# RWKV-7 chunk recurrence: the identity products of the state are taken out of TensorE, and VectorE adds a decayed copy of the state instead

## What is computed

```python
def step(s, inp):
    w_t, k_t, v_t, kk_t, a_t = inp[:5]
    sa = jnp.einsum('bhvk,bhk->bhv', s, kk_t)
    s = (s * w_t[:, :, None, :]
         - sa[..., None] * (kk_t * a_t)[:, :, None, :]
         + v_t[..., None] * k_t[:, :, None, :])
    y = jnp.einsum('bhvk,bhk->bhv', s, inp[5]) if len(inp) > 5 else None
    return s, y
```

## Time and profile before

| | us |
|---|---|
| median of three runs | 5098.99 (5093.28 to 5112.98) |
| profiled execution, its own time | 5105.09 |
| its span, first to last instruction | 5103.3 |
| around the span | 1.8 |
| granted TensorE clock, mean | 0.970 |
| TensorE busy (MATMUL) / weight loads | 4705.9 (92%) / 2817.4 (55%) |
| VectorE / ScalarE / GpSimd busy | 2535.0 (50%) / 1836.3 (36%) / 1383.1 (27%) |
| rwkv, 3107 to 4823 us: TensorE / VectorE busy | 1569.6 / 927.4 of 1716 |

### The profile page before, as it was taken

How to read it: one execution, slowest core, us unless ns; L and a number is a source line. 1 busy time by engine, 2 the same in 40 slices (tenths; PEclk the granted TensorE clock), 3 DMA queues, 4 the chain that set the end, 5 groups by cost and what they waited for, 6 DMA issues and landing times. The chain is left out here.

```text
span 5103.3 us, 123816 instructions
## 1 busy us (share of the span) xinstructions
PE 4705.9 (92%) x50814; PEld 2817.4 (55%) x50814; DVE 2535.0 (50%) x4204; ACT 1836.3 (36%) x4413; POOL 1383.1 (27%) x2884
## 2 busy tenths in 40 slices
PE   6999997999999998999999969899999989989699
PEld 3666663333333334454444437777787777778544
DVE  2444444665666661232343355555555555555376
ACT  1212111444444431132222225455555555555332
POOL 1111111333332320000000005444454444445343
PEclk8999997999999998999999989999999999999899
DMA  5222223000000005432322246666666666666575
GB/s 210 95 83 93 85 75 120 5 23 24 24 24 24 23 6 220 146 135 63 124 74 69 66 129 172 166 169 173 171 183 171 158 178 171 181 165 167 154 229 174
DMA packets 958460, 602.74 MB, mean 118 GB/s; under 512 B 661382, under 2 KB 903686, under 8 KB 943881
## 3 DMA queue, kind: packets, MB, share of 16 engines
q1 hardware_dynamic: 871434, 572.86, 38.3%
q10 hardware_dynamic: 86528, 22.82, 2.1%
HBM read 398.63 MB, written 196.88 MB: 117 GB/s over the span
## 5 line engine op out<-in xcount | busy, mean ns | idle before, releaser
L934 PE MATMUL at_bS<-at_qT,at_kT 97*64 97x512 f32 (+1 forms) x2368 | 604.9, 596 | 15.1 <-ACT at_pT L1032 14.5
L1639 PE MATMUL p_bU<-keep_hT,p_slab 128*128 128x512 f32 (+1 forms) x1504 | 588.6, 554 | 8.0 <-DMA p_slab<-in_o_w_in_dram 7.4
L1069 DVE TENSOR_REDUCE at_mx<-at_bM 128x1 f32<-128x512 f32 (+1 forms) x656 | 394.0, 627 | 352.2 <-PE at_bM L899 351.2
L2216 PE MATMUL rw_bank<-keep_rw_hg,rw_slab 128*128 128x256 f32 x2048 | 481.5, 389 | 8.9 <-DMA keep_rw_hg<-scratch_hT 6.9
L1032 ACT ACTIVATE at_pT<-at_bS 128x512 f32<-128x512 f32 (+1 forms) x592 | 342.4, 591 | 396.8 <-PE at_bS L934 377.3
L1639 PEld LDWEIGHTS p_bU<-keep_hT,p_slab 128*128 128x128 f32 x1504 | 286.6, 191 | 305.7 <-issue 288.4
L2216 PEld LDWEIGHTS rw_bank<-keep_rw_hg,rw_slab 128*128 128x128 f32 x2048 | 382.5, 192 | 69.3 <-DMA keep_rw_hg<-scratch_hT 7.7
L2519 DVE TENSOR_TENSOR rw_S<-rw_bank,rw_dec 128x128 f32<-128x128 f32 x288 | 83.0, 288 | 649.3 <-PE rw_bank L2196 644.0
L2021 POOL TENSOR_TENSOR rw_g_at<-rw_g_at,rw_g_prod 64x14 f32<-64x14 f32 (+6 forms) x1008 | 328.6, 326 | 79.0
L856 POOL TENSOR_TENSOR at_sum_pool<-at_sum_pool,at_pT 128x512 f32<-128x512 f32 x192 | 244.0, 1271 | 372.2 <-ACT at_pT L1032 354.8
L2019 POOL TENSOR_TENSOR rw_g_prod<-rw_g_at 64x14 f32<-64x14 f32 (+6 forms) x1008 | 321.3, 319 | 79.1
(11 more groups left out here) (289 smaller groups left out, 9926.4 us busy)
## 6 DMA issues: line engine op xcount, KB each, us to landing
keep_wide<-scratch_heads SPq DMA_DIRECT2D x144, 512.0 KB
keep_rw_hg<-scratch_hT SPq DMA_DIRECT2D x64, 1024.0 KB
rw_XB<-scratch_inverses SPq DMA_DIRECT2D x576, 64.0 KB
keep_wide<-scratch_lora SPq DMA_DIRECT2D x144, 128.0 KB
scratch_bv<-rw_bv SPq DMA_DIRECT2D x144, 128.0 KB
scratch_products<-rw_NB SPq DMA_DIRECT2D x288, 64.0 KB, 4.0
scratch_y<-rw_ysb ACTq DMA_DIRECT2D x288, 64.0 KB, 4.4
scratch_heads<-p_z SPq DMA_DIRECT2D x17, 1024.0 KB, 4.9
```

Source lines behind the costliest of these rows:

```text
L934: last = pe.matmul(bS[rows, g % 3, 0:nq * P], kT[:, s, k * P + VH * x:k * P + VH * x + VH], qT[:, s, q0 * P:(q0 + nq) * P], start=True, st ...
L1069: nc.vector.tensor_reduce(mx[:, j, piece:piece + 1], bM[:, (FIRST_ITEM[b] + i) % 2, 0:n], AX.X, ALU.max).then_inc(max_red, 1)
L1639: last = pe.matmul(bU[:, n % 4, 0:w], slab[:, i, k, :], hT[:, k, tok:tok + w], start=(k == 0), stop=(k == KD - 1))
L2216: last = pe.matmul(DENSE[:, GT * j:GT * (j + 1)], slab[:, j, q, :], hg[:, x.slot, q, :], start=(q == 0 and j == 0), stop=(q == KD - 1), sk ...
```

## The change

The products with the identity are taken out of `step_begin`, so that SU holds only what the chunk adds. A second tile `Sd` holds the state times the decay of the coming chunk: `decay_state` (new, one 128x128 tensor-tensor instruction) makes it behind each carry, behind a wait for that carry's own semaphore, and `carry` becomes two scalar-tensor-tensor instructions of 128x64 (one for each direction, its decay a per-partition scalar): S = SU times decay + Sd. The waits for the decays move from carry 0 to `decay_state(…, 0)`, which stands behind carry 3 of the body before.

```diff
-        S = core.sb("S", [P, 2, C])
+        S, Sd = core.sb("S", [P, 2, C]), core.sb("S_decayed", [P, 2, C])
...
-        set_up, par_done = sem("rw_setup"), sem("rw_params")
+        set_up, par_done, sd_done = sem("rw_setup"), sem("rw_params"), sem("rw_state_decayed")
...
                         for rows, other in ACROSS:
-                            pe.matmul(SU[rows, C * d:C * d + C], ident[rows, rows], S[rows, d, :],
-                                      start=False, stop=False, skip_group_check=True)
                             pe.matmul(Y[other, C * d:C * d + C], AR[rows, n.six, d, u, 1, :], S[rows, d, :],
                                       start=False, stop=False, skip_group_check=True)
...
                 def carry(n, c):
 
+                    v.wait_ge(sd_done, 4 * n.n + c + 1)
+                    v.wait_ge(su_mm, 4 * n.n + c + 1)
+                    for d in range(2):
+                        last = nc.vector.scalar_tensor_tensor(out=S[:, d, :], in0=SU[:, C * d:C * d + C], scalar=dec[:, n.kept, d, c:c + 1],
+                                                              in1=Sd[:, d, :], op0=ALU.mult, op1=ALU.add)
+                    last.then_inc(s_out, 1)
+
+                def decay_state(n, c):
+
                     if c == 0:
                         v.wait_ge(dec_part, 2 * n.n + 2)
                         if n.group == NG - 1:
                             v.wait_ge(dec_last, n.pair + 1)
-                    v.wait_ge(su_mm, 4 * n.n + c + 1)
-                    nc.vector.tensor_tensor(S[:], SU[:, 0:2 * C].rearrange("p (d v) -> p d v", d=2),
-                                            dec[:, n.kept, :, c, None].broadcast_to([P, 2, C]), ALU.mult).then_inc(s_out, 1)
+                    v.wait_ge(s_out, 4 * n.n + c)
+                    nc.vector.tensor_tensor(Sd[:], S[:], dec[:, n.kept, :, c, None].broadcast_to([P, 2, C]), ALU.mult).then_inc(sd_done, 1)
...
                     if has[0]:
                         carry(n, 0)
+                        decay_state(n, 1)
...
                     if has[0]:
                         carry(n, 1)
+                        decay_state(n, 2)
                     query_taps(n.on(-1))
...
                     if has[0]:
                         carry(n, 2)
+                        decay_state(n, 3)
...
                     if has[0]:
                         carry(n, 3)
+                    if has[1]:
+                        decay_state(m, 0)
                     if has[4]:
                         weights(l)
                         queries(l)
```

## The result

The changed kernel takes 5119.70 us in the median of 20 runs, the kernel before, run beside it, 5103.45: a ratio of 1.0025, interval 1.0018 to 1.0032. It is slower, as forecast, but by 0.25% in place of 0.7%, and the ratio lies inside the 0.5% that I had called no difference. The profiled executions are 5121.65 and 5105.09, 16.6 us apart. Of these, 5.2 lie ahead of the first `step_end` of rwkv (3107.4 against 3112.6 us), where nothing was changed: over the fourteen profiled executions of this document that point lies anywhere from 3102.8 to 3117.1. Rwkv itself, from its first to its last `step_end`, grew by 10.2 us.

The account below looks back on a forecast made before the run. VectorE's chains at two places of a body were taken to hold up TensorE. +35.4 + 26.0 - 15.2 - 10 = +36 us on 5105.1 gave 5141, less 6.1 to the median: 5135 us, range 5095 to 5168.

Parts of the forecast that it names:

- the two places: Chunk 0's `step_sa` and the scores behind chunk 2's `step_begin`, where VectorE releases TensorE's next instruction.
- Instruction supply: TensorE's 61 "issue" stops, 73.7 us: fewer matmuls (4 us) and new waits (6 us) relieve them, -10 us.
- Place A: Ahead of chunk 0's `step_sa`: copy and longer carry delay VectorE's chain 0.52 us in 68 bodies, +35.4 us.
- the moved wait for the decays: Wait for `dec_part` moves up a body's quarter, to decays made two bodies earlier: costs nothing.
- Inside the same wait: Chunk 0's first R1 product gets S 0.19 us later, hidden in the wait ahead of `step_sa`: no added cost.
- Place B: Scores behind chunk 2's `step_begin`: carry 1 and its copy delay taps and mask 0.52 us, 50 bodies, +26.0 us.
- Chunk 1: Same-half tiles are fuller there, so removing identity products saves 0.22 us in 69 bodies, -15.2 us.
- chunks 0, 2 and 3: Removing identity products gains nothing: chunk 0 then waits for VectorE, in chunks 2 and 3 crossing tiles stay full.
- rival 2: Carry and copy delay VectorE only 0.28 to 0.40 us: 5107 to 5121, no measurable difference; chance 0.20.
- The tiles as the bound: TensorE's same-half tiles bound the stage and VectorE has room: 63 us saved, 5036, faster; chance 0.10.
- The small delay: Same as rival 2: VectorE delay of 0.28 to 0.40 us, 5107 to 5121; chance 0.20.
- The dear end: VectorE delay of 0.63 us, without chunk 1's gain or the supply's relief: +74 us, 5173; chance 0.10.

Follow-up runs that it names:

- e1: Changed kernel with the identity products back and the carry adding zeros, keeping the longer carries and copies: 5162.7 us, ratio 1.0115 to the kernel before.
- e2: Kernel before without the identity products, old single-instruction carry, no copy, output not the reference's: 5060.0 us, ratio 0.9913 to the kernel before.
- p2: Changed kernel with 128 TensorE instructions run once ahead of the first body, shifting block boundaries: 5144.5 us, ratio 1.0071 to the kernel before.
- e5: Changed kernel with the `decay_state` calls of chunks 0 and 2 moved off the two places: 5083.3 us, ratio 0.9948 to the kernel before.
- e3: Kernel before with 64 more TensorE instructions per body, ahead of chunk 0's `step_sa`: 5102.8 us, ratio 1.0009 to the kernel before.
- e4: Changed kernel with 64 more TensorE instructions per body, ahead of chunk 0's `step_sa`: 5132.0 us, ratio 1.0054 to the kernel before.

## Why the prediction was right or wrong, point by point

The direction, the two places and the sign of each term were right; the size was wrong, and with it the step from the sum to a chance of 0.63 for a measurable loss.

**The step that failed is the term "Instruction supply", -10 us with 0 and -25 as its ends.** It measured -41, outside its own bounds. It had two parts. The new waits were priced at 6 us, half a microsecond for a fifth of the stops; e1, which has the waits and all the instructions, has 25 us fewer stops. The instructions taken out were priced at 4 us, by their 6% share; the rest of the give-back, 16 us, came with them (29 in e2, which has no new waits). The second scaling assumed that stops are spread evenly over the instructions. They are not: three quarters of their time lies in the 7 us of a body from chunk 1's `step_end` to chunk 3's `step_sa`, where small products stand densest, and where a block ends in it matters too (p2). What a wait does to the loading of the blocks no row shows.

The Trainium skill, Runtime: NRT & Kernel Launch, section "Instruction fetch mechanics", has the loading mostly hidden. That holds for most blocks here (37 stops of over 0.6 us for 301 packets), but what isn't hidden is 74 us, 4% of the stage.

**Place A, +0.52 us, measured +0.73**: 0.26 in the start of chunk 0's R1, 0.47 behind it. The pair of scalar-tensor-tensor took 0.48 as priced (278 ns each). The rest, in about equal parts, is that the copy starts 0.11 behind the carry and not 0.04 (median of 68 bodies against 0.03 for the copies of the other chunks), that the carry itself starts 0.07 later behind the product it waits for, and that the instruction behind the copy is slower, 0.12. The first two have one wait more than what they are compared with, for the decays and for the copy, and carry 0, which had a second wait before the change too, does not start later. The prediction had put the moved wait for the decays at nothing. It came in nearly every body, 70 waits, 89.9 us; I had said near 80. "Inside the same wait" was right of the late R1, in that e5 moved the copy alone and place A gave 0.48 back.

**Place B, +0.52, measured +0.59**, over 44 waits where 50 were forecast.

**Chunk 1, -0.22, measured -0.19**; chunks 0, 2 and 3, nothing, measured nothing: a regular body of e2 differs from before in chunk 1 (-0.15 and -0.05) and otherwise only in the places that wait for VectorE (-0.05 at place A, +0.11 at place B).

**The sum by the measured terms**: 68 x 0.73 + 50 x 0.59 - 69 x 0.19 = +66 us; less 41 of stops, +25. Rwkv grew by 10.2 between its first and last `step_end`; the rest of the 16.6 between the profiled executions lies mostly ahead of it. So 15 us of the sum are not assigned. The medians of regular bodies times 68 and 50 overstate the delays where a stop or another wait already stood in a body: the mean of place B's stretch grew by 0.47 us where its median grew by 0.59.

**The rule on own semaphores.** The Trainium skill, VectorE: DVE Perf Modes, section "The DRAIN you can't avoid", measured no extra cost for a semaphore behind each instruction. By that rule, as the prediction worked it out, the copy would start 0.08 ahead of the carry's end. The trace does not agree for these short instructions: the copy starts 0.04 behind it at place B and 0.11 at place A. The measured time is in rival 2's 5107 to 5121, but came there by another way: the delay was larger than forecast, not smaller.

**The rivals.** The tiles as the bound: out, by e2. The small delay: out, by the rows above, though its time is the measured one. The dear end had the delays right: 68 x 0.73 + 50 x 0.59 = +79 us against its +74. What it left out, chunk 1's gain (-13) and the supply's relief (-41), both came. The direction was right by the delays, but that the time came out so near no change is the mis-sized supply term, and in part the position of the blocks, which nobody chose.

## What to carry to other kernels

Where an engine's trace has stops that nothing releases, look at the instruction queue's packets first. Here nearly every stop of over 0.6 us ends 1.15 to 1.80 us behind a packet, and the price of an instruction depends on where it stands: taking 64 a body out of the chunks gave 41 us where the regular bodies show 10 (e2), and 64 put into a wait cost 1.5 and 12 us (e3, e4). Work that is taken off a full engine has to be put where the other engine idles, not just behind the instruction that makes its input: two calls moved turned this change from 0.25% slower to 0.5% faster than the kernel before, and two more orders made it 1.1%. A difference of 0.5% between two long unrolled kernels can be the position of block boundaries alone; a shift by half a block ahead of the stage tells (0.46% between p2 and the changed kernel).

## What the runs showed of the hardware

- TensorE's instructions come in packets of 16 KB, 256 instructions; 382 of 383 stops of over 0.6 us end 1.15 to 1.80 us behind the end of such a packet, which takes about 1 us. Most stops lie where a block of small products lasts about 3.5 us; at which length they set in was not measured. 128 instructions that run once cost 25 us by shifting the boundaries.
- A scalar-tensor-tensor of 64 columns with a pointer scalar, one input in PSUM, takes 278 ns; a tensor-tensor of 128 columns from SBUF 292 (mean in e5) to 307 (mean in the changed kernel), the old carry from PSUM 288.
- A VectorE instruction that waits for its own forerunner's semaphore starts 0.04 us behind its end (0.11 with a further wait, at `decay_state` of chunk 0 in the changed kernel), and without such a wait 0.08 ahead.
